# A decoder trunk's expert stage: the refill of a weight buffer is issued before, instead of behind, two activation stores

## The reference, cut to what matters

```python
def peer_ffn(h, w_q, key1, key2, u, v):
    ...
    q = (hf @ w_q).reshape(T, PEER_HEADS, 2, PEER_HALF)
    s1 = jnp.einsum('thd,nd->thn', q[:, :, 0], key1)
    s2 = jnp.einsum('thd,nd->thn', q[:, :, 1], key2)
    v1, i1 = lax.top_k(s1, PEER_TOPK)
    v2, i2 = lax.top_k(s2, PEER_TOPK)
    ...
    top, sel = lax.top_k(cand, PEER_TOPK)
    eid = jnp.take_along_axis(cidx, sel, axis=-1)
    gate = jax.nn.softmax(top.astype(jnp.float32), axis=-1).astype(h.dtype)
    ...
        ug = u[ec]
        act = jax.nn.gelu(jnp.einsum('td,thkd->thk', xc, ug), approximate=False)
        return jnp.einsum('thk,thkd->td', gc * act, v[ec])
```

## Time and profile before

| what | value |
|---|---|
| median of 3 runs | 2814.96 us (2812.17 to 2815.4) |
| profiled execution, its own time | 2812.17 us |
| its span, first to last instruction | 2810.4 us |
| TensorE busy / weight loads | 97% / 88% |
| VectorE / ScalarE / GpSimd busy | 80% / 41% / 20% |
| TensorE's granted clock, mean | 0.99 of full speed |
| SP's DMA queue | 58.4% of 16 engines' span |
| U stage of the first layer | from about 655 to 1049 us |
| U stage of the second layer | from about 2038 to 2431 us |

### The profile page before, as it was taken

One profiled execution on the slowest core, in us unless ns is written; L12 is line 12 of the kernel. 1 busy time (PEld: TensorE's weight loads), 2 busy tenths in 40 slices (PEclk: granted clock), 3 DMA queues, 4 the chain that ended last, 5 costly groups with the idle time before them and its releaser, 6 DMA issues.

```text
span 2810.4 us, 51269 instructions
## 1 busy us (share of the span) xinstructions
PE 2724.6 (97%) x19786; PEld 2472.4 (88%) x19786; DVE 2239.4 (80%) x4318; ACT 1162.8 (41%) x1664; POOL 567.1 (20%) x354
## 2 busy tenths in 40 slices
PE   6999998999999999999999999999999999999998
PEld 6998887889999997787799988788999999987776
DVE  7998686579977658888879987756899766688887
ACT  4543422244554443333355343222455444433334
POOL 0000002110877730000000000030227686100000
PEclk9999999999999999999999999999999999999999
DMA  7553360466788778788745534434578887888885
GB/s 299 181 189 124 134 220 11 158 240 212 219 247 248 197 233 303 279 281 282 246 151 190 184 106 187 135 116 151 187 227 240 242 232 204 271 280 281 291 284 189
DMA packets 258985, 593.81 MB, mean 211 GB/s; under 512 B 82608, under 2 KB 198064, under 8 KB 200240
## 3 DMA queue, kind: packets, MB, share of 16 engines
q1 hardware_dynamic: 192656, 572.74, 58.4%
q0 software_dynamic: 36864, 0.15, 2.7%
q10 hardware_dynamic: 29216, 17.57, 2.1%
HBM read 537.27 MB, written 53.08 MB: 210 GB/s over the span
## 4 chain that ended last, share of the span: by engine, by line
PE 83%; DVE 11%; ACT 2%; issue 1%; DMA 1%; POOL 0%; DVEq 0%; SPq 0%; POOLq 0%; ACTq 0%
PE ps L1197 26%; PE ps L1176 20%; PE ps L687 13%; PE ps L649 6%; PE ps L777 2%; PE ps L1186 2%; DVE u_lo L2113 2%; PE ps L727 1%; PE ps L1062 1%; DMA ring<-in_stream 1%; PE ps L939 1%; DVE region L1721 1%; PE ps L1009 1%; DVE region L2164 1%; PE ps L996 1%
## 5 line engine op out<-in xcount | busy, mean ns | idle before, releaser
L1176 PE MATMUL ps<-h_hi,u_hi 128*128 128x256 f32 x2048 | 580.5, 283 | 3.3 <-DVE u_lo L2113 3.0
L1176 PE MATMUL ps<-h_lo,u_hi 128*128 128x256 f32 x2048 | 571.5, 279 | 0.0
L1176 PE MATMUL ps<-h_hi,u_lo 128*128 128x256 f32 x2048 | 570.9, 279 | 0.0
L2360 POOL DMA_INDIRECT gate_rows<-route x256 | 475.2, 1856 | 291.9 <-DVE route L2227 124.7
L2113 DVE TENSOR_TENSOR u_lo<-ring,u_hi 128x1024 fp32r<-128x1024 f32 x256 | 312.3, 1220 | 180.9 <-ACT u_hi L1513 169.1
L1176 PEld LDWEIGHTS ps<-h_hi,u_hi 128*128 128x128 f32 x2048 | 384.8, 188 | 7.1 <-DVE u_lo L2113 6.5
L1176 PEld LDWEIGHTS ps<-h_hi,u_lo 128*128 128x128 f32 x2048 | 384.2, 188 | 0.0
L1176 PEld LDWEIGHTS ps<-h_lo,u_hi 128*128 128x128 f32 x2048 | 384.0, 188 | 0.0
L1534 ACT ACTIVATE u_hi<-ring 128x1024 fp32r<-128x1024 f32 x192 | 203.9, 1062 | 323.7 <-PE ps L1197 323.7
L2120 DVE TENSOR_TENSOR u_lo<-ring,u_hi 128x1024 fp32r<-128x1024 f32 x192 | 234.7, 1223 | 50.9 <-ACT u_hi L1534 50.7
L1513 ACT ACTIVATE u_hi<-ring 128x1024 fp32r<-128x1024 f32 x256 | 269.3, 1052 | 0.0
(11 more groups left out here) (394 smaller groups left out, 5189.7 us busy)
## 6 DMA issues: line engine op xcount, KB each, us to landing
ring<-in_stream SPq DMA_DIRECT2D x456, 1024.0 KB, 7.6
act_rows<-region SPq DMA_DIRECT2D x256, 128.0 KB
gate_rows<-rstd ACTq DMA_DIRECT2D x2, 8192.0 KB, 29.6
region<-gate_rows SPq DMA_DIRECT2D x256, 64.0 KB, 3.9
region<-act_rows SPq DMA_DIRECT2D x128, 128.0 KB, 4.3
small_inverse<-act_rows SPq DMA_DIRECT2D x128, 128.0 KB, 4.2
gate_rows<-route POOLq DMA_INDIRECT x256
region<-in_c SPq DMA_DIRECT2D x7, 512.0 KB, 5.7
```

Source lines behind the costliest of these rows:

```text
L1176: ins = mm(ps[:, c % 4, 0:T], x, y[:, k, :], start=k == 0 and i == 0, stop=k == KD - 1 and i == 2)
L2360: gp.indirect_dma_start(gate_cells, bass.IndirectOffsetOnAxis(ap=gate_at[:, r:r + 1].bitcast(I32), axis=0), gate_weight[:, r:r + 1], None, ...
```

## The change

In `load_beside_acts` the load of block n is issued straight behind the wait in `passed`, before the stores of the finished activations. Nothing is added or removed. Each call issues the same wait, the same load and the same stores.

```diff
                     nonlocal stored_acts
                     passed(n - SLOTS)
+                    load(n)
                     upto = 2 * sum(m <= n - SLOTS for m in U_AT) - 3
                     for c in range(stored_acts, upto):
                         store_act(c)
                     stored_acts = max(stored_acts, upto)
-                    load(n)
```

## The result

| | before | after |
|---|---|---|
| median, same chip | 2815.18 us (2812.17 to 2817.84, 6 runs) | 2834.89 us (2831.38 to 2843.38, 6 runs) |
| span of the profiled execution | 2810.4 us | 2835.5 us |

The ratio is 1.0081, with a 95% interval of 1.0066 to 1.0095. It is estimated over all executions on record (31 of the changed kernel, with a median of 2837.32 us) and is not the quotient of the two medians above, which differ by 19.7 us, a ratio of 1.0070. The two profiled executions differ by 25.1 us. My forecast of 2826 us, 11 us over the median, had the sign, the range and one of the two causes that I had named, but only about half of the size.

A forecast was written before the change was run, and what follows sets the result against it. VectorE was taken to set the pace in the selection stretch, TensorE in the gate stretch. Selection and handoff, 2 x (2.8 + 4.2) = 14.0 us, on the profiled 2812.2 us gave 2826 us, range 2815 to 2836.

The forecast's parts named there:

- The load 1.0 us earlier: U stage: issuing the ring load 1.0 us earlier gains 0, since nobody waits for it.
- The store is held by the load in front: U-stage turns: a store queued behind the 1 MB load lands 5.1 to 5.9 us after turn start, at most 7.75.
- Rival 2: Stores slip past the load and land as before; everything stays, 2812 to 2815 us; chance 0.10.
- rival 3: At the ring, the earlier load gains up to 1.00 us a turn, no lower than 2803 us; chance 0.05.
- The price of one late landing: Selection stretch: cover reaches 6.15 us after turn start t0; a landing at 7.75 costs 1.6 us.
- the selection term: Selection stretch and the turn ahead of it: late stores cost 1.6 plus 1.2, together 2.8 us a layer.
- The early turns: Turn at 685.97, ahead of the selection stretch: VectorE's lag carried into it, taken as 1.2 us a layer.
- The turns from 710 to 770: Selection stretch, 11 turns: 1.6 us a layer, one late turn or several small ones, between 0 and 7.7.
- the handoff term: Handoff: late stores hold gelu(121) and stop TensorE before scores(124), 4.2 us a layer (2.2 to 5.4).
- The gate stretch: 802 to 1026 us: gelu starts 6.76 us after turn start, later than a normal landing; costs 0.
- Rival 4: Selection stretch: delay locks in, every two turns 1.4 us longer, 7.7 us a layer; total 2840 us; chance 0.08.
- Rival 1: Only the handoff costs, 2 x 2.2 to 2 x 4.4 us, giving 2817 to 2821 us; chance 0.20.

The follow-up runs named there:

- Six slots: Changed order with the activation buffer six slots deep instead of four, gelu(c) waiting for store c-6, against the kernel before: 2814.23 us, ratio 0.9996.
- own queue: Load first, stores issued by ScalarE on its own DMA queue, each behind the next u_high, against the kernel before: 2814.87 us, ratio 0.9996.
- Turns 1 to 8 alone: Load first only in turns 1 to 8 of the U stage, old order elsewhere, against the kernel before: 2820.24 us, one execution.
- handoff: Load first only in the four handoff turns (blocks of V), old order in the U stage's turns, against the kernel before: 2828.09 us, ratio 1.0033.
- Stage alone: Load first only in the U stage's turns, old order at the handoff, against the kernel before: 2834.61 us, ratio 1.0069.

## Why the prediction was right in kind and short in size

**The load 1.0 us earlier is worth 0: right.** "Six slots" and "own queue" have it and stand at 0.9996.

**The store is held by the load in front: right.** The Trainium skill's rule in "DMA: Bandwidth & Descriptors", section "Queues, rings and completion order", which the prediction weighed, agrees with the trace: in the changed kernel the store at 721.00 lands 7.45 us later, and the fastest of both stages after 4.4 us, where before the change the median was 1.9. Rival 2 is refuted, and rival 3 with it. The Trainium skill's advice in "DMA: Bandwidth & Descriptors", section "Rules for kernel authors", to issue a DMA early, brought a loss here, since the load's gain of a microsecond was paid by the stores behind it in the same queue.

**The price of one late landing: right.** I had put the cover in the selection stretch at t0 + 6.15. The changed kernel, SP's turn, ScalarE, VectorE and TensorE:

```profile
720.61 0.34 SPq L522 DMA_DIRECT2D ring<-in_stream  x1
721.00 0.91 SPq L526 DMA_DIRECT2D act_rows<-region  x2
...
728.47 0.39 ACT L1541 ACTIVATE region<-ps 128x256 f32<-128x256 f32 x1 [5.45 <-DMA act_rows<-region]
...
729.83 1.23 DVE L2113 TENSOR_TENSOR u_lo<-ring,u_hi 128x1024 fp32r<-128x1024 f32 x1 [1.82 <-ACT u_hi L1513]
...
731.11 0.39 PE L1176 MATMUL ps<-h_hi,u_hi 128*128 128x256 f32 x1 [1.87 <-DVE u_lo L2113]
```

gelu(21) starts at t0 + 7.86, 1.7 us past the cover, and VectorE stands 1.82 us. I had 1.6 for a landing at 7.75.

**Failed: the selection term, "2.8 us a layer".** It measured 10.5 and 11.4 at c = 60. The mechanism was the one I had described; how often it strikes, and in which stretches, was not. Its parts:

- *How often a landing is late.* I took 5.1 to 5.9 us after the turn's start as normal, from one load, and 7.75 as a rare bound, "one such turn". The loads of the changed kernel, 655 to 1026 us:

```profile
L522 SPq DMA_DIRECT2D ring<-in_stream x63: 333/343/346, 658.4 to 1024.0; - x63
...
DMA to landing us min/median/max: 4.8/5.5/7.3
```

  The median is what I assumed. The tail isn't rare: read from the semaphore events of single DMAs, 22 of the 126 loads of both stages land over 6.15 us after their issue. By the same reading it is 25 of 128 in the trace of before (a rougher reading, as more than half of these loads lack some of their 16 events). The kernel before had that tail, and it was hidden, as its stores stood ahead of the load.
- *The early turns, "I take 1.2".* The lag at c = 19 is 3.7 and 4.5. I looked at one turn there, the one at 685.97. The stage starts with too little lead for an earlier turn, of 671.45, as well:

```profile
677.27 0.38 ACT L1541 ACTIVATE region<-ps 128x256 f32<-128x256 f32 x1 [4.25 <-PE ps L1176]
...
681.54 0.38 ACT L1541 ACTIVATE region<-ps 128x256 f32<-128x256 f32 x1
...
682.90 1.23 DVE L2113 TENSOR_TENSOR u_lo<-ring,u_hi 128x1024 fp32r<-128x1024 f32 x1 [1.90 <-ACT u_hi L1513]
...
684.18 0.19 PEld L1176 LDWEIGHTS ps<-h_hi,u_hi 128*128 128x128 f32 x1 [1.38 <-DVE u_lo L2113]
```

  gelu(5) starts at 677.27 instead of 674.54. The row names TensorE as what it waited for, but the store issued at 671.83 lands at 677.26, 5.4 us after its issue. This is an ordinary landing, and it stops TensorE for 1.4 us at c = 9. Then a landing of 6.3 us makes u_lo(14) late (696.99), and 2.0 us are lost from c = 15 to 18. Turns 1 to 8 alone cost 5.3 us in either layer.
- *The turns from 710 to 770, "1.6 us a layer".* The lag grows by 3.0 and 3.1 from c = 19 to 42. One stop in layer one, at 731.11, is near the size that I gave, and something follows it that I had not counted (1.3 us at half clock, last section). Layer two has two stops there, of 1.1 and 1.3 us.
- *The turns from 774 to 825, no term at all.* The lag grows by 3.8 us in both layers. VectorE was busy 28.7 of 30 us from 772 to 802 us before the change, with `decode` between the u_low's, the steps that work out the picks' numbers (lines 2207 to 2214, 1.1 to 2.3 us each). The early turns have the same steps, for the other half of the tokens. In the changed kernel:

```profile
786.17 0.34 SPq L522 DMA_DIRECT2D ring<-in_stream  x1
786.56 2.62 SPq L526 DMA_DIRECT2D act_rows<-region  x2
...
794.37 0.39 ACT L1541 ACTIVATE region<-ps 128x256 f32<-128x256 f32 x1 [4.77 <-DMA act_rows<-region]
...
795.74 1.23 DVE L2113 TENSOR_TENSOR u_lo<-ring,u_hi 128x1024 fp32r<-128x1024 f32 x1 [2.69 <-ACT u_hi L1513]
...
797.01 0.39 PE L1176 MATMUL ps<-h_hi,u_hi 128*128 128x256 f32 x1 [1.41 <-DVE u_lo L2113]
```

  The landing at t0 + 8.2 gives a stop of 1.6 us. So the cover there is about t0 + 6.6, nearly the 6.8 of the gate stretch, but the gate stretch proper also has u_low's lead and this one has none. I drew the border of the free stretch at 802 us because TensorE did not stop there before, which says nothing of its reserve. The last stop of the group, of 0.9 us, ends at 827.30 and so lies inside the stretch that I had put at 0.

**Failed the other way: the handoff term, "4.2".** It measured 0 in the changed kernel. Its mechanism is real (6.2 and 12.4 us in the profiled execution of "handoff"), but it needs SP to be held up by the scatter, and in the changed kernel SP isn't:

```profile
1030.55 0.34 SPq L522 DMA_DIRECT2D ring<-in_stream  x1
...
1032.11 0.48 SPq L598 DMA_DIRECT2D prm<-in_prm  x1
...
1037.09 0.34 SPq L522 DMA_DIRECT2D ring<-in_stream  x1
...
1044.40 0.39 ACT L1541 ACTIVATE region<-ps 128x256 f32<-128x256 f32 x1 [3.09 <-DMA act_rows<-region]
```

The parameters' load follows 1.6 us behind the last turn's load, where it was 5.4 us before the change (1020.92 to 1026.31). The scatter is no longer what SP waits for, because the whole U stage is 10 us behind by then. gelu(121) still waits 3.1 us for its store, which TensorE doesn't feel. "Stage alone", whose handoff has the old order, has nearly the whole span of the changed kernel (24.3 of 25.1 us over before), so behind the stage's stops the new order at the handoff costs next to nothing. I had added terms that exclude each other: with a selection term of 10 us, the handoff's had to go.

**The gate stretch, 0: right from c = 60 on** (about 830 us before the change), in all runs: between c = 60 and 110 no lag moves by as much as 0.1 us. Its first chunks belong to the item above.

**Rival 4**, in which the delay locks in, gave 7.7 us for the tight stretch and 2840 us. Its total is nearer than its mechanism: the 710 to 770 turns lost 3 us, and most landings between two late ones are normal. Rival 1 had it the wrong way round: of the two terms it was the handoff that cost nothing.

**The sum.** With the measured terms it is 2812.2 + 10.5 + 11.1 + 0 = 2833.8 us, and 3.5 us of other differences between the two executions make up 2837.3, the profiled execution's own time. Mine had one more slip. Its 14.0 us were added to 2812.2 us, the fastest of the three executions, and the total was named as if it were a median. Added to the median it would have been 2829 us, and the named 2826 forecasts a change of only 11 us.

## What to carry to other kernels

A DMA that frees a slot must not be queued behind a large one where its landing has no cover, even if the large one then starts earlier: look at who waits for each of the two, and if both must be early, make the buffer deeper, or issue the small one as soon as its data are there. Another queue by itself is not shown to be enough. Take a transfer's landing from all of its instances, its slowest fifth above all, and compare that with the cover in every stretch, the ones without a stop too. Before adding the costs of two places, ask whether the delay at the first one removes the condition of the second.

## What the runs showed of the hardware

**A stop of TensorE can be followed by half clock.** TensorE's last matmul before the stop in the changed kernel ends at 729.24, the next one starts at 731.11, and the clock falls at 732.5. Stretches of 1 us behind that stop, columns as in the earlier trace rows:

```profile
731.00:732.00 1.00, 0.89 (x7) 0.89 (x8) 0.97 (x6) 0.02 (x1) 0.69 (x2) 1.00 1.03 201
...
733.00:734.00 1.00, 1.00 (x6) 1.00 (x6) 1.00 (x3) 0.41 (x2) 0.70 (x2) 0.50 0.40 13
...
736.00:737.00 1.00, 1.00 (x11) 1.00 (x11) 1.00 (x5) 0.94 (x1) 1.00 (x1) 1.00 0.65 262
```

The granted clock is 0.50 (1.2 GHz) for 3.4 us, and 6 or 7 matmuls fit into a microsecond instead of the 11 at 1.00. That is the additional lag of 1.3 us at c = 25 in layer one. The stop at the same place in layer two was shorter (1.1 us) and had no such fall, and neither had that of "stage alone" in layer one, which was nearly as long (1.7 us of lag, ended at 732.40). In the handoff kernel the clock fell after both stops, for 3.4 us and, in the stop of 10 us, for 10.2 us, and scores(125) lost 1.6 and 2.3 us more:

```profile
2431.00:2432.00 1.00, 0.00 (x0) 0.00 (x0) 0.00 (x0) 0.00 (x0) 0.00 (x0) 1.00 1.09 312
2433.00:2434.00 1.00, 0.00 (x0) 0.00 (x0) 0.00 (x0) 0.00 (x0) 0.00 (x0) 0.50 0.91 352
2440.00:2441.00 1.00, 1.00 (x6) 1.00 (x6) 0.94 (x1) 0.00 (x0) 0.00 (x0) 0.50 0.76 82
```

TensorE's last matmul had ended at 2427.94, 4.7 us before the clock fell at 2432.6.

**Where the slow landings come from is open.** Single DMA packets of both kernels show fetches of instructions: 16 KB ones (the page's q8, 160 packets and 2.62 MB in a run), every 12 to 19 us in the first U stage, and 8 KB ones (q14, 0.73 MB). In the changed kernel 64 of the 126 loads have one of either kind between issue and landing, and all 22 loads over 6.15 us are among them (20 with one of 16 KB). The 62 others land after 5.40 us in the median and 6.02 at most. In the kernel before, 2 of the 25 loads over 6.15 us have none. That is a correlation: no run moved the fetches.
